# Five packed transfers instead of four at a kernel's start, and a warm-up of eight matmuls instead of nine

## The reference

```python
def hybrid_layer(x, g_mix, w_in, sinks, w_a, w_b, w_out, g_mlp, w_up, w_down):
    B, S, _ = x.shape
    pos = jnp.arange(S)
    h = rmsnorm(x, g_mix)
    z = h @ w_in                   # 256 x 1024 by 1024 x W_IN
    ...
```

## Time and profile before

| | us |
|---|---|
| median of 3 runs | 992.79 |
| lowest and highest of them | 992.38, 992.85 |
| the profiled execution's own time | 992.89 |
| its span | 991.1 |
| PE busy | 984.2 |
| DVE busy | 732.6 |
| ACT busy | 497.3 |
| POOL busy | 129.8 |

### The profile page before, as it was taken

How to read it: one execution, slowest core, us unless ns; L and a number is a source line. 1 busy time by engine, 2 the same in 40 slices (tenths; PEclk the granted TensorE clock), 3 DMA queues, 4 the chain that set the end, 5 groups by cost and what they waited for, 6 DMA issues and landing times.

```text
span 991.1 us, 13299 instructions
## 1 busy us (share of the span) xinstructions
PE 984.2 (99%) x5502; PEld 835.6 (84%) x5502; DVE 732.6 (74%) x836; ACT 497.3 (50%) x596; POOL 129.8 (13%) x101
## 2 busy tenths in 40 slices
PE   9999999999999999999999999999999999999997
PEld 8888888888888888888888888888887899899796
DVE  5867786776656656677786777888877777789984
ACT  6545553554444345444563454444478554644252
POOL 0000000000000000000000030000000159169720
PEclk9999999999999999999999999999999999999999
DMA  9897796546655564697796667555554965345451
GB/s 362 300 280 266 234 281 209 197 168 212 197 185 170 185 216 132 192 300 247 234 273 219 222 176 243 200 184 207 170 173 153 300 193 173 126 170 155 112 191 43
DMA packets 116764, 204.33 MB, mean 206 GB/s; under 512 B 10209, under 2 KB 29665, under 8 KB 116449
## 3 DMA queue, kind: packets, MB, share of 16 engines
q1 hardware_dynamic: 116704, 203.50, 62.8%
HBM read 189.09 MB, written 12.06 MB: 203 GB/s over the span
## 4 chain that ended last, share of the span: by engine, by line
PE 99%; DVE 0%; ACT 0%; DVEq 0%; issue 0%; ACTq 0%
PE bank L887 13%; PE bank L889 13%; PE bank L890 13%; PE bank L1219 12%; PE bank L910 10%; PE bank L914 9%; PE bank L921 9%; PE bank L1223 6%; PE bank L1301 2%; PE bank L1512 1%; PE bank L1001 1%; PE bank L1091 1%; PE bank L919 1%; PE bank L912 1%; PE bank L1499 1%; PE bank L1173 1%
## 5 line engine op out<-in xcount | busy, mean ns | idle before, releaser
L1988 DVE TENSOR_TENSOR w_lo<-arena,w_hi 128x2048 fp32r<-128x2048 f32 (+1 forms) x79 | 181.5, 2309 | 80.5 <-ACT w_hi L1600 80.1
L1988 DVE TENSOR_TENSOR w_lo<-raw,w_hi 128x2048 fp32r<-128x2048 f32 (+1 forms) x78 | 178.1, 2293 | 70.3 <-ACT w_hi L1600 69.9
L1600 ACT ACTIVATE w_hi<-raw 128x2048 fp32r<-128x2048 f32 (+1 forms) x83 | 157.0, 1892 | 93.2 <-PE bank L890 63.8
L1600 ACT ACTIVATE w_hi<-arena 128x2048 fp32r<-128x2048 f32 (+1 forms) x79 | 149.4, 1891 | 97.7 <-PE bank L890 72.7
L1219 PE MATMUL bank<-hT,w_hi 128*128 128x512 f32 x504 | 123.4, 391 | 0.0
L1219 PEld LDWEIGHTS bank<-hT,w_hi 128*128 128x128 f32 x504 | 92.2, 188 | 17.6
L887 PE MATMUL bank<-w_hi,hT 128*128 128x512 f32 (+1 forms) x240 | 91.9, 383 | 0.0
L2688 POOL TENSOR_TENSOR rstd<-mean,const 128x1 f32<-128x1 f32 (+1 forms) x16 | 9.1, 578 | 628.0 <-DVE mean L1997 458.9
L889 PE MATMUL bank<-w_lo,hT 128*128 128x512 f32 (+1 forms) x224 | 85.5, 381 | 0.0
L890 PE MATMUL bank<-w_hi,hT 128*128 128x512 f32 (+1 forms) x224 | 85.5, 381 | 0.0
L887 PE MATMUL bank<-w_hi,uT_hi 128*128 128x512 f32 x208 | 81.1, 390 | 0.0
(11 more groups left out here) (339 smaller groups left out, 1854.4 us busy)
## 6 DMA issues: line engine op xcount, KB each, us to landing
arena<-in_w_in SPq DMA_DIRECT2D x21, 1024.0 KB, 5.3
raw<-in_w_in SPq DMA_DIRECT2D x20, 1024.0 KB, 7.0
arena<-in_w_up SPq DMA_DIRECT2D x16, 1024.0 KB, 5.7
raw<-in_w_up SPq DMA_DIRECT2D x16, 1024.0 KB, 5.8
arena<-in_w_down SPq DMA_DIRECT2D x16, 1024.0 KB, 5.1
raw<-in_w_down SPq DMA_DIRECT2D x16, 1024.0 KB, 5.1
raw<-in_e_w_in SPq DMA_DIRECT2D x6, 1024.0 KB, 5.5
arena<-in_e_w_in SPq DMA_DIRECT2D x6, 1024.0 KB, 5.3
```

Source lines behind the costliest of these rows:

```text
L1600: act.activation(w_hi[:, p % SPLIT_RING, :, 0:n], raw_at(p)[:, :, 0:n], copy).then_inc(hi_ready, 1)
L1988: dve.tensor_tensor(w_lo[:, s, :, 0:n], raw_at(p)[:, :, 0:n], w_hi[:, s, :, 0:n].bitcast(F32), ALU.subtract).then_inc(lo_ready, 1)
```

## The change

`FIRST_PARTS` has five entries instead of four, so the packed array is cut into five transfers. Sizes in KiB for all 128 partitions (the first also carries the gains): before 516, 768, 768, 1024; after 388, 512, 640, 768, 768. A new semaphore `fourth_landed` stands for the fourth. The waits on ACT, DVE and PE are moved to fit: blocks 4 and 5 of the weights are now split together, as 6 and 7 already were, and PE runs uppers, lowers and remainders of 4 and 5 as pairs. `WARM` goes from 9 to 8.

```diff
-WARM = 9
-FIRST_PARTS = (((0, 1), (0,)), ((2, 3), (1, 2)), ((4, 5), (3, 4)), ((6, 7), (5, 6, 7)))
+WARM = 8
+FIRST_PARTS = (((0,), (0,)), ((1, 2), (1,)), ((3,), (2, 3)), ((4, 5), (4, 5)), ((6, 7), (6, 7)))
...
                     first_part(1).then_inc(second_landed, 16)
+                    first_part(2).then_inc(raw_landed[0], 16)
...
-                    first_part(2).then_inc(raw_landed[0], 16)
-                    first_part(3).then_inc(raw_landed[1], 16)
+                    first_part(3).then_inc(fourth_landed, 16)
+                    first_part(4).then_inc(raw_landed[1], 16)
...
-                pe.wait_ge(first_turned, 4)
                 pe.wait_ge(first_hi, 3)
                 upper(2)
-                pe.wait_ge(turned_lo, 2)
+                pe.wait_ge(first_turned, 4)
                 lower_of(2)
                 pe.wait_ge(first_lo, 3)
                 remainder_of(2)
 
+                pe.wait_ge(first_turned, 5)
                 pe.wait_ge(hi_ready, 1)
                 upper(3)
+                pe.wait_ge(turned_lo, 2)
                 lower_of(3)
...
                 upper(4)
+                upper(5)
                 pe.wait_ge(turned_lo, 3)
                 lower_of(4)
+                lower_of(5)
                 pe.wait_ge(second_lo, 1)
                 remainder_of(4)
-
-                pe.wait_ge(second_hi, 2)
-                upper(5)
-                lower_of(5)
-                pe.wait_ge(second_lo, 2)
                 remainder_of(5)
...
+            act.wait_ge(raw_landed[0], 16)
             act.activation(w_hi[:, 0, 2, :], first_w(2), copy).then_inc(first_hi, 1)
-            act.wait_ge(raw_landed[0], 16)
             act.activation(w_hi[:, 0, 3, :], first_w(3), copy).then_inc(hi_ready, 1)
+            act.wait_ge(fourth_landed, 16)
             first_rows(4)
             first_rows(5).then_inc(turned_hi, 3)
-            act.activation(w_hi[:, 1, 0, :], first_w(4), copy).then_inc(second_hi, 1)
+            act.activation(w_hi[:, 1, 0:2, :], first_w(4, 2), copy).then_inc(second_hi, 1)
             act.wait_ge(raw_landed[1], 16)
-            act.activation(w_hi[:, 1, 1, :], first_w(5), copy).then_inc(second_hi, 1)
...
-            first_upper(1).then_inc(first_turned, 1)
+            dve.wait_ge(second_landed, 16)
+            first_upper(1)
+            first_upper(2).then_inc(first_turned, 1)
             dve.wait_ge(first_turned, 3)
             first_lower(1).then_inc(turned_lo, 1)
-
-            dve.wait_ge(second_landed, 16)
-            first_upper(2)
-            first_upper(3).then_inc(first_turned, 1)
             dve.wait_ge(first_hi, 2)
             first_remainder(1, 1).then_inc(first_lo, 1)
-            dve.wait_ge(first_turned, 4)
-            first_lower(2)
-            first_lower(3).then_inc(turned_lo, 1)
+            first_lower(2).then_inc(first_turned, 1)
+
+            dve.wait_ge(raw_landed[0], 16)
+            first_upper(3).then_inc(first_turned, 1)
             dve.wait_ge(first_hi, 3)
             first_remainder(2, 1).then_inc(first_lo, 1)
-
+            dve.wait_ge(first_turned, 5)
+            first_lower(3).then_inc(turned_lo, 1)
             dve.wait_ge(hi_ready, 1)
             first_remainder(3, 1).then_inc(lo_ready, 1)
+
             dve.wait_ge(turned_hi, 3)
             first_lower(4)
             first_lower(5).then_inc(turned_lo, 1)
             dve.wait_ge(second_hi, 1)
-            first_remainder(4, 1).then_inc(second_lo, 1)
-
-            dve.wait_ge(second_hi, 2)
-            first_remainder(5, 1).then_inc(second_lo, 1)
+            first_remainder(4, 2).then_inc(second_lo, 1)
+
```

More of the change, by code:

```diff
@@ L414, in build_program @@
         second_landed = sem("second_landed")
+        fourth_landed = sem("fourth_landed")
         first_turned = sem("first_turned")
```

## The result

The changed kernel took 994.58 us in the median of 22 executions (992.85 to 1001.37), the kernel before 992.68 in 22 (992.29 to 993.13). The ratio over all executions is 1.0032 with a 95% interval of 1.0020 to 1.0045; that of the medians is 1.0019, and the difference is the tail. So there are two things to explain: the fastest execution after is 0.56 us slower than the fastest before, and 7 of 22 lie above 999 while none of before passes 993.2.

A forecast was written before the change was run, and what follows sets the result against it. PE (TensorE), busy 984.2 of 991.1 us, was taken to bound the kernel. The first product 0.31 us earlier was worth 0.17 us, other parts nothing: 992.79 - 0.17 gives 992.6 us, range 992.1 to 993.1.

The forecast's parts named there:

- the first landing: Kernel start: the first packed transfer, 131 KB smaller, lands 0.31 us earlier, at 4.05 instead of 4.36 us.
- the first product: Start of PE's products: begins at 4.82 us instead of 5.13, bound by w_hi of block 0; worth 0.17 us.
- A fifth transfer: Packed transfers at the start: one more was taken to cost 0, with 0.5 us as the upper bound.
- The recorded 1.3 us of stall: Packed transfers: fixed part of about 2 us charged in series, fifth landing near 12.6 us, estimate 994.0.
- the recorded table: First products: when PE needs each operand against when it is ready; least cover 0.7 us.
- The rival of a late rise: PE's start: longer pause before the first product restarts the clock's count, rise at 10.8 us, 994.4 us; chance 0.08.
- The rival of an early rise: PE's start: clock rises early in many executions, so data holds PE; median near 992.35 us; chance 0.13.
- the term of the landings: Packed transfers after the first: 2.45 ns a KiB from 4.05 us, landings at 5.30, 6.87, 8.75 and 10.63.
- The table of covers: First products: PE's need against readiness, such as upper 2 at 8.7 (ready 7.5); no stops expected.
- The cover I called the least: Uppers 4 and 5 on PE: needed at 11.4 us, ready at 10.7, a cover of 0.7 us.
- only two things can move the time: Whole kernel: only the first product's start and PE's speed in its first microseconds can change the time.
- the cut costs nothing by itself: Warm-up: eight matmuls leave PE free at about 4.6 us, before the data at 4.82, at no cost.

The follow-up runs named there:

- e2: The changed kernel with nine warm-up matmuls again instead of eight: median 993.35 us beside 992.36 before.
- e10: The changed kernel with nine warm-up matmuls and the second packed transfer's rows padded from 4096 to 4128 bytes: 992.47 us beside 992.65 before.
- e3: The kernel before with its last packed transfer cut in two, so five transfers with the first three as before: 992.38 us beside 992.36.
- e9: The kernel before with eight warm-up matmuls ahead of the first product and the ninth after the third pair of products: 992.70 us beside 992.65.
- e1: The kernel before with eight warm-up matmuls instead of nine, nothing else: median 992.39 us beside 992.36, highest 999.18.
- e15: The kernel before with eight warm-up matmuls and the first GLU weight load issued one small transfer later: 992.58 us beside 992.55.
- e12: The changed kernel with its eight warm-up matmuls and a ninth after the third pair of products: 993.25 us beside 992.65 before.
- e8: The kernel before with six warm-up matmuls instead of nine: median 995.85 us beside 992.60, highest 1001.91.

## Why the prediction was wrong

**What held.** In the profiled execution the first landing (3.89 for 4.05), the second (5.17 for 5.30) and the first product (4.67 for 4.82) came near what was worked out. That is in part luck: the same first transfer landed between 3.64 (e2) and 4.31 (e10) in the other kernels that have it unpadded, so 0.31 us off 4.36 was one draw of a wide spread. A fifth transfer costs nothing: e3 has it and takes 992.38 beside 992.36, with its last landing at 10.74 for 10.63. The Trainium skill, DMA: Bandwidth & Descriptors (Anatomy of one DMA), gives a transfer on the GpSimd path a fixed part of about 2 us; these are issued by SP, and e3 says that no such part adds up over queued transfers. The recorded 1.3 us of stall for that case is 2.0 less the cover of 0.7 at blocks 4 and 5, which hang on the fourth transfer and not on the fifth at 12.6; with the fifth alone 2 us late the recorded table gives 0.5.

The rival of a late rise, by which a longer pause makes the chip count anew, is out. e9 has the longer pause (0.86 us), its products are 0.23 us apart from 6.2 us on, and its time is that of before. The executions of the change over 999 us point the same way: by 0.47 us lost for each us at the low level, 6.6 us would need 14 us of it and a mean granted clock of 0.993 or less, and three of the seven list 0.998, which executions at 993 have too. The rival of an early rise came true in this profile (4.2 us) and hid part of the loss.

**The step that failed first** is the term of the landings: 2.45 ns a KiB of the bytes ahead, which put the third at 6.87. It measured 8.23, 8.00, 8.17, 8.23, 8.33 and 8.02 in six kernels with that cut, 1.1 to 1.5 us over. The rate was read from transfers 1.88 us apart, in which the 16 engines end within 0.6 us of each other (packet records of the second to fourth); it is the rate of the sum, and the landing is that of the last engine. In the change the first engine was done with the third transfer by 6.06 us and the last at 7.85. That the engines are full, as in the earlier trace rows, didn't hold with the new cut: in the eight late kernels one to five of them had no packet for a while between 4.25 and 6 us. The table of covers gave remainder 2 and upper 2 a microsecond (7.5 for 8.7); with the high clock already at 4.7 us, as in the profiled execution, PE is there at 7.8, so 1.1 us of the delay became a wait. The cover I called the least, 0.7 at uppers 4 and 5, wasn't the one that gave way first. This is 0.6 to 1.0 us of the 1.9.

**The step that was missing** is a price for the shorter warm-up outside the start. The prediction held that "only two things can move the time", both at the start, and "the cut costs nothing by itself" was argued from where the matmuls stand in time. What it changed was the length of PE's program, and with it when the next block of instructions is fetched, 900 us on, beside a load that has a cover of 2.5 us. e1, e9 and e15 show it: with eight alone the load lands 9.8 us after its issue and 3 of 10 executions are over 1, with the program's length or the load's place restored it lands after 6.9 and 7.2 and 1 of 11 each is over 1, none over 1.8. In the change itself the profiled execution had the issue of 1.51 us and the load on time; that the load is late in those over 999 us is inferred from e12, which takes them away, and from e8's profile. None of those was profiled.

**Consequence.** I had no rival in which an edit at the start acts in a stage that it doesn't touch, and gave slower by over 0.2% a chance of 0.03.

## What to carry to other kernels

A transfer that is waited for lands when the slowest of the 16 DMA engines is done (8.23 here, where fifteen had finished by 6.49): take its landing from rows of transfers cut in the same way, and leave a cover of a microsecond and more where a cut is new. After any edit that changes how many instructions an engine runs, look at the thinnest cover anywhere behind it, and at the spread of the executions, not at the median and one profile alone. A tail can be told from a shift by making each half of an edit alone: here the transfers made the shift and the warm-up the tail.

## What the hardware did that was not expected

One DMA engine out of 16 ended 1.4 us behind the rest after 1.5 MiB: by the packet records it had none in hand until 5.53 us, then one of 0.973 us and seven of 0.196. The mean share over 4.36 to 6.25 us still reads 1.00; in 4.25 to 5.25 us it reads 0.92, and 0.81 in e2. A load of 1 MiB among small transfers took 6.0 to 6.8 us to its last packet, or 8.8 to 11.0, by whether its issue had taken 1.2 us or 0.6. PE's clock fell to 0.50 at 940.3, in an idle stretch from 938.1 to 942.8, and stayed there until 947.2, so a wait of 4.7 us cost more than itself. The moment at which products go from 0.43 to 0.23 us apart differs between executions: about 7.1 us in the profile of before, ahead of the first product at 4.67 in that of the change. The granted clock's high level begins at 4.0 to 7.2 us in 19 of the 20 profiles, and at 8.5 in that of e8, with six warm-up matmuls and 1.5 us of pause.
